# Sliding-window attention in head pairs: eight TensorE jobs per key-value head in place of 26

## The chip, the cores and the metric

The kernel runs on one core of one Trainium2 chip. The metric is the time of one execution in device microseconds (us), as the median of several runs. TensorE does matrix products, VectorE (DVE in the profile) and ScalarE (ACT) do elementwise work and read TensorE's results out of PSUM, GpSimd (POOL) does some elementwise work, and SyncE (SP) issues the DMAs.

## What is computed

One layer of a decoder trunk on 256 tokens of width 2048: a gated DeltaNet branch and a sliding-window attention branch run side by side, are merged by gates, and an MLP follows. The change is in the attention branch alone. Its 32 query heads share 4 key-value heads, 8 to each:

```python
scores = jnp.einsum("bnqkgd,bnskd->bnkgqs", qb, kb).astype(f32) * (SWA_HEAD_DIM ** -0.5)
...
scores = jnp.where(valid[None, :, None, None], scores + bias, -jnp.inf)
sink = sinks.astype(f32).reshape(SWA_KV_HEADS, G)[:, :, None, None]
m = jnp.maximum(scores.max(axis=-1, keepdims=True), sink)
p = jnp.exp(scores - m)
probs = (p / (p.sum(axis=-1, keepdims=True) + jnp.exp(sink - m))).astype(v.dtype)
o = jnp.einsum("bnkgqs,bnskd->bnqkgd", probs, vb)
```

A head is 64 channels wide. The window is 128 tokens, so for one head the 256 queries see three 128x128 blocks of keys: block 0 on itself, block 1 on block 0, block 1 on itself.

## The kernel before

The whole program is one long stream of dense products on TensorE. `output` forms one 256x512 piece of a projection out of 8 (or 16) weight chunks. A chunk is 256x512 weights, loaded by SyncE into a ring of four, then split by ScalarE and VectorE into a high part (`w_hi`, line 648) and a low part (`w_lo`, line 988), three chunks ahead of its use. For each chunk TensorE makes twelve products (lines 288 to 290), six for each of the two 128-row halves. After each half `output` calls a job function with a counter `h`. This counter is the **slot**: a job that belongs to slot h is put into TensorE's stream behind the six products of that slot, and into ScalarE's and VectorE's streams at the same h, behind the split of the chunk that comes three later.

In the stage that the change touches, `mix1`, a loop of four turns over the key-value heads j, each turn is two outputs (a gate projection and the branch product of DeltaNet), which is 32 slots and 192 products, and the attention of the eight heads s of key-value head j is done by `swa_step` in these slots. For one head it has five links:

- **scores** in slot `SCORE[s]`: products 128x128 and 128x256 into PSUM bank `pb` = s mod 2 of `J` (lines 466 and 467). The queries of an even head lie in partitions 0 to 63, those of an odd one in 64 to 127, and each uses the half of the array with those rows.
- VectorE adds the distance bias and takes the maxima (`bias_done`, `negm_done`, lines 1167 to 1174); ScalarE takes the exponentials with their sums (`exps_done`, lines 799 to 802).
- **transposes** in slot `PTURN[s]`: three transposes of `prob` into bank 2 (line 475), which ScalarE copies to `probT` (`pT_copied`, line 805).
- **values** in slot `PV[s]`: three products into bank 3 (lines 483 to 485).
- after an odd head, VectorE divides both heads' results by the sums into `oS` (line 1183, `oS_done`).

Slot 3 transposes the queries of all eight heads (`qfix`), slot 31 the results (`oS`), each by eight transposes (line 317). So TensorE has 3 x 8 + 2 = 26 jobs for each key-value head. Their slots are SCORE = 4, 6, 9, 12, 14, 17, 20, 22; PTURN = 9, 11, 14, 17, 19, 22, 25, 27; PV = 13, 14, 19, 20, 24, 25, 29, 30. Some slots hold two or three of them, and 18 slots of the 32 hold one at least.

The projections use float32r operands (one instruction for each product); the attention's products are float32, of which the trace shows two instructions for each (except for the transposes).

Of the kernel before, what the change touches and what calls it, by code (L numbers as in the profile page):

```python
# [20 lines left out]
ALU = mybir.AluOpType  # L21
ACT = mybir.ActivationFunctionType
F32 = mybir.dt.float32
F32R = mybir.dt.float32r
AX_X = mybir.AxisListType.X

P = 128
T = 256
NT = T // P
# [6 lines left out]
C = 64  # L36
NCH = T // C
U = NT * HG
HQ = 8
# [33 lines left out]
ROWS, TK, TQ, KKQ, INV, QTM, OT = 11, 16, 21, 22, 25, 40, 63  # L73
P1, P2, P3 = (40, 45, 50, 55), (42, 47, 52, 57), (44, 49, 54, None)

SCORE = tuple(4 + 8 * s // 3 for s in range(8))
PTURN = tuple(h + 5 for h in SCORE)
PV = tuple(SCORE[s | 1] + 8 - (s + 1) % 2 for s in range(8))


def hybrid_trunk(nc, x, weights, w_ba, colp_d, rowp_d, masks_d, dist_d, fgain_d, out):
    with ExitStack() as ctx:
# [26 lines left out]
        with ExitStack() as mixers:  # L109
# [17 lines left out]
            with ExitStack() as swa:  # L127
# [4 lines left out]
                qTs = sb("qTs", [P, 4, T], where=swa)  # L132
                kfix = sb("kfix", [P, T], where=swa)
# [132 lines left out]
        def _(pe):  # L266
# [181 lines left out]
            def swa_step(h, j):  # L448
                if h == 3:

                    pe.wait_ge(qfix_done, j + 1)

                    pe.wait_ge(fix_done, j + 1)
                    turn_group(qfix, 0, q_T)
                for s in range(HQ):
                    r = slice((s % 2) * C, (s % 2) * C + C)
                    pb = s % 2
                    if h == SCORE[s]:
                        if s == 0:
                            pe.wait_ge(qT_a, j + 1)  # L460
                            pe.wait_ge(qT_d, j + 1)
                            pe.wait_ge(fix_done, j + 1)
                        if s >= 2:

                            pe.wait_ge(bias_done, HQ * j + (s - 1))
                        mm(J[:, pb, 0:P], qTs[r, s // 2, 0:P], kfix[r, 0:P], start=True, stop=True)  # L466
                        mm(J[:, pb, P:3 * P], qTs[r, s // 2, P:T], kfix[r, 0:T], start=True,  # L467
                           stop=True).then_inc(score_done, 1)
                    if h == PTURN[s]:

                        pe.wait_ge(exps_done, HQ * j + (s + 1))
                        if s:
                            pe.wait_ge(pT_copied, HQ * j + s)
                        for i in range(3):
                            ins = tr(J[:, 2, i * P:(i + 1) * P], prob[:, pb, i * P:(i + 1) * P], ident)  # L475
                        ins.then_inc(p_T, 1)
                    if h == PV[s]:
                        pe.wait_ge(pT_copied, HQ * j + (s + 1))

                        if s and s % 2 == 0:  # L480
                            pe.wait_ge(oS_done, HQ // 2 * j + s // 2)
                        o = J[:, 3, (s % 4) * P:(s % 4 + 1) * P]
                        mm(o[:, 0:C], probT[:, pb, 0:P], vfix[:, 0], start=True, stop=True)
                        mm(o[:, C:P], probT[:, pb, P:2 * P], vfix[:, 0], start=True, stop=False)
                        mm(o[:, C:P], probT[:, pb, 2 * P:3 * P], vfix[:, 1], start=False, stop=True).then_inc(pv_done, 1)
                if h == 31:
                    pe.wait_ge(oS_done, HQ // 2 * (j + 1))
                    turn_group(oS, 0, oS_T)

            def decay_step(h):  # L490
# [145 lines left out]
        def _(act):  # L636
# [146 lines left out]
            def swa_step(h, j):  # L783
                if h == 0:

                    act.wait_ge(sq_d, 4)
                    act.wait_ge(sq_a, 4)
                    A(qfix[:], xres[:, :, bass.ds(j * NB, NB)], ACT.Copy).then_inc(qfix_done, 1)
                if h == 3:
                    act.wait_ge(q_T, j + 1)  # L790
                    A(qTs[:, 0:2], J[:, 0].rearrange("p (a t) -> p a t", a=2), ACT.Copy).then_inc(qT_a, 1)
                for s in range(HQ):
                    pb = s % 2
                    if h == SCORE[s]:
                        act.wait_ge(negm_done, HQ * j + (s + 1))

                        if s >= 2:
                            act.wait_ge(p_T, HQ * j + (s - 1))
                        A(prob[:, pb, 0:P], sbuf_s[:, pb, 0:P], ACT.Exp, bias=negm[:, s, 0:1], accum_out=lsum[:, s, 0:1])
                        A(prob[:, pb, P:3 * P], sbuf_s[:, pb, P:3 * P], ACT.Exp, bias=negm[:, s, 1:2],  # L800
                          accum_out=lsum[:, s, 1:2])
                        A(esink[:, s], negm[:, s], ACT.Exp, bias=slf[:, 1, s:s + 1]).then_inc(exps_done, 1)
                    if h == PTURN[s]:
                        act.wait_ge(p_T, HQ * j + (s + 1))
                        A(probT[:, pb], J[:, 2, 0:3 * P], ACT.Copy).then_inc(pT_copied, 1)
                if h == 31:
                    act.wait_ge(oS_T, j + 1)
                    for b in range(2):
                        ins = A(os_hi[:, bass.ds(j * 4 + 2 * b, 2), :], J[:, b].rearrange("p (a t) -> p a t", a=2), ACT.Copy)
                    ins.then_inc(os_hi_done, 1)  # L810
# [167 lines left out]
        def _(dve):  # L978
# [167 lines left out]
            def swa_step(h, j):  # L1146
                if h == 0:

                    dve.wait_ge(kT_done, 1)
                    dve.wait_ge(kv_d, 1)  # L1150
                    V.tensor_copy(kfix[:], kT[:, bass.ds(j, 1), :].rearrange("p a t -> p (a t)"))
                    V.tensor_copy(vfix[:], vs[:, :, bass.ds(j * C, C)])
                    V.tensor_copy(slf[:], rowp[:, 64:128].rearrange("p (a n) -> p a n", a=2)[:, :, bass.ds(j * HQ, HQ)]).then_inc(fix_done, 1)
                if h == 3:
                    dve.wait_ge(q_T, j + 1)
                    V.tensor_copy(qTs[:, 2:4], J[:, 1].rearrange("p (a t) -> p a t", a=2)).then_inc(qT_d, 1)
                for s in range(HQ):
                    pb = s % 2
                    if h == SCORE[s]:
                        dve.wait_ge(score_done, HQ * j + (s + 1))  # L1160
                        if s == 0:
                            dve.wait_ge(fix_done, j + 1)
                            dve.wait_ge(dist_in, 16)
                        if s >= 2:

                            dve.wait_ge(exps_done, HQ * j + (s - 1))
                        stt(out=sbuf_s[:, pb], in0=dist[:], scalar=slf[:, 0, s:s + 1], in1=J[:, pb, 0:3 * P],
                            op0=ALU.mult, op1=ALU.add).then_inc(bias_done, 1)
                        dve.wait_ge(bias_done, HQ * j + (s + 1))
                        V.tensor_reduce(r3[:, s], sbuf_s[:, pb].rearrange("p (a k) -> p a k", a=3), AX_X, ALU.max).then_inc(max_link, 1)  # L1170
                        dve.wait_ge(max_link, j * (2 * HQ) + (2 * s + 1))
                        tt(r3[:, s, 1:2], r3[:, s, 1:2], r3[:, s, 2:3], ALU.max).then_inc(max_link, 1)
                        dve.wait_ge(max_link, j * (2 * HQ) + (2 * s + 2))
                        ts(negm[:, s], r3[:, s, 0:2], slf[:, 1, s:s + 1], -1.0, ALU.max, ALU.mult).then_inc(negm_done, 1)
                    if h == PV[s] and s % 2:

                        i, pair = s // 2, slice(s - 1, s + 1)
                        dve.wait_ge(pv_done, HQ * j + (s + 1))
                        tt(lsum[:, pair], lsum[:, pair], esink[:, pair], ALU.add).then_inc(l_link, 1)
                        dve.wait_ge(l_link, j * HQ + (2 * i + 1))  # L1180
                        V.reciprocal(lsum[:, pair], lsum[:, pair]).then_inc(l_link, 1)
                        dve.wait_ge(l_link, j * HQ + (2 * i + 2))
                        tt(oS[:, :, (s - 1) * C:(s + 1) * C].rearrange("p t (s c) -> p s t c", s=2),
                           J[:, 3, (s - 1) % 4 * P:((s - 1) % 4 + 2) * P].rearrange("p (s t c) -> p s t c", s=2, t=NT),
                           lsum[:, pair].unsqueeze(3).broadcast_to([P, 2, NT, C]), ALU.mult).then_inc(oS_done, 1)
                if h == 31:
                    dve.wait_ge(os_hi_done, j + 1)
                    for b in range(2):
                        ins = tt(os_lo[:, bass.ds(j * 4 + 2 * b, 2), :], J[:, b].rearrange("p (a t) -> p a t", a=2),
                                 os_hi[:, bass.ds(j * 4 + 2 * b, 2), :].bitcast(F32), ALU.subtract)  # L1190
                    ins.then_inc(os_lo_done, 1)
# [350 lines left out]
```

## Time and profile before

| what | value |
|---|---|
| median of 3 runs | 1968.29 us (1958.04 to 1972.9) |
| the profiled execution, its own time | 1963.88 us |
| its span, first to last instruction | 1962.1 us |
| TensorE busy | 1906.0 us, 97% of the span |
| VectorE busy | 1104.8 us, 56% |
| ScalarE busy | 882.7 us, 45% |
| mean granted clock of TensorE, as a share of full speed | 0.988 |
| the four turns of the stage | 726 to 975 us |

The profiled execution's time is 1.8 us over its span, and 4.4 us under the median of the runs. TensorE's busy time says that it nearly always has a matmul in the array; since matmuls are pipelined, what one costs the stream is read from one start to the next, not from the duration printed.

### The profile page before, as it was taken

What the parts mean: (1) busy time and instruction counts of PE and PEld (TensorE: products, weight loads), DVE (VectorE), ACT (ScalarE), POOL (GpSimd) and SP (SyncE); (2) the same over time, 40 slices, a digit from 0 to 9 for tenths busy, and PEclk for the clock granted to TensorE, in tenths of its full rate; (3) what the DMA queues carried; (4) which work ended last, traced back from release to release, by engine and by line L of the source; (5) the groups of instructions that cost most, each with busy time, mean ns of one, the idle gap of its engine ahead of it and who ended that gap; (6) DMA issues with size and microseconds to landing.
All of it is one profiled execution on the core that took longest, in us unless ns stands there. A gap on an engine that the chain in (4) does not pass through costs nothing.

```text
span 1962.1 us, 29288 instructions
## 1 busy us (share of the span) xinstructions
PE 1906.0 (97%) x10816; PEld 1563.9 (80%) x10816; DVE 1104.8 (56%) x1470; ACT 882.7 (45%) x1398; POOL 120.5 (6%) x86
## 2 busy tenths in 40 slices
PE   7998998998999999999999999999999999999997
PEld 6887877877877888777888888888888888888886
DVE  5366676676676555656555555555554445554444
ACT  5344345354354345455444445444443344444442
POOL 0004014014023000000000000000000000000000
PEclk9899999999999999999999999999999999999999
DMA  6343333333333354344456655555555555555553
GB/s 249 118 165 119 115 130 108 119 119 118 108 127 114 115 165 140 120 138 139 148 194 205 204 200 208 183 184 189 184 192 193 194 192 181 186 188 188 192 195 125
DMA packets 87953, 316.36 MB, mean 161 GB/s; under 512 B 9648, under 2 KB 10160, under 8 KB 87728
## 3 DMA queue, kind: packets, MB, share of 16 engines
q1 hardware_dynamic: 86992, 312.64, 47.2%
q0 software_dynamic: 576, 2.10, 0.3%
q8 instruction: 78, 1.28, 0.2%
q10 hardware_dynamic: 288, 0.18, 0.0%
q14 instruction: 19, 0.16, 0.0%
HBM read 312.79 MB, written 2.10 MB: 160 GB/s over the span
## 4 chain that ended last, share of the span: by engine, by line
PE 54%; issue 38%; DVE 3%; POOL 3%; ACT 1%; DMA 0%; DVEq 0%; ACTq 0%; POOLq 0%; SPq 0%
PE acc L288 15%; PE acc L290 13%; PE acc L289 13%; PE J L385 4%; PE J L433 1%; PE J L317 1%; POOL rg L1406 1%; PE J L424 1%; PE J L467 1%; ACT w_hi L648 1%; PE J L466 1%; PE J L441 1%; DVE cT L1043 1%; DVE qn L1043 1%; PE J L475 1%
## 5 line engine op out<-in xcount | busy, mean ns | idle before, releaser
L988 DVE TENSOR_TENSOR w_lo<-raw,w_hi 128x1024 fp32r<-128x1024 f32 x584 | 724.7, 1243 | 665.8 <-ACT w_hi L648 663.7
L648 ACT ACTIVATE w_hi<-raw 128x1024 fp32r<-128x1024 f32 x584 | 618.3, 1060 | 647.0 <-PE acc L290 645.0
L288 PE MATMUL acc<-w_hi,hT_hi 128*128 128x512 f32 x1440 | 584.6, 406 | 8.4 <-DVE hT_lo L1006 4.5
L290 PE MATMUL acc<-w_hi,hT_lo 128*128 128x512 f32 x1440 | 565.2, 393 | 0.0
L289 PE MATMUL acc<-w_lo,hT_hi 128*128 128x512 f32 x1440 | 565.1, 392 | 0.0
L288 PEld LDWEIGHTS acc<-w_hi,hT_hi 128*128 128x128 f32 x1440 | 272.4, 189 | 74.6 <-issue 11.4
L290 PEld LDWEIGHTS acc<-w_hi,hT_lo 128*128 128x128 f32 x1440 | 272.4, 189 | 59.0
L289 PEld LDWEIGHTS acc<-w_lo,hT_hi 128*128 128x128 f32 x1440 | 272.8, 189 | 52.1 <-issue 1.0
L288 PE MATMUL acc<-w_hi,act_hi 128*128 128x512 f32 x512 | 199.3, 389 | 0.0
L290 PE MATMUL acc<-w_hi,act_lo 128*128 128x512 f32 x512 | 199.2, 389 | 0.0
L289 PE MATMUL acc<-w_lo,act_hi 128*128 128x512 f32 x512 | 199.2, 389 | 0.0
L290 PEld LDWEIGHTS acc<-w_hi,act_lo 128*128 128x128 f32 x512 | 96.1, 188 | 20.1
L288 PEld LDWEIGHTS acc<-w_hi,act_hi 128*128 128x128 f32 x512 | 96.1, 188 | 20.0
L289 PEld LDWEIGHTS acc<-w_lo,act_hi 128*128 128x128 f32 x512 | 96.1, 188 | 19.6
L288 PE MATMUL acc<-w_hi,og_hi 128*128 128x512 f32 x256 | 104.3, 407 | 0.0
L290 PE MATMUL acc<-w_hi,og_lo 128*128 128x512 f32 x256 | 100.2, 391 | 0.0
L289 PE MATMUL acc<-w_lo,og_hi 128*128 128x512 f32 x256 | 99.9, 390 | 0.0
L385 PEld LDWEIGHTS J<-mats 64*64 64x64 f32 x2048 | 66.5, 140 | 24.9 <-issue 24.9
L385 PE MATMUL J<-mats 64*64 64x64 f32 x2048 | 72.6, 226 | 10.6 <-POOL mats L1428 10.6
L288 PEld LDWEIGHTS acc<-w_hi,og_hi 128*128 128x128 f32 x256 | 48.1, 188 | 12.6 <-issue 4.0
L290 PEld LDWEIGHTS acc<-w_hi,og_lo 128*128 128x128 f32 x256 | 48.1, 188 | 10.8
L289 PEld LDWEIGHTS acc<-w_lo,og_hi 128*128 128x128 f32 x256 | 48.2, 188 | 8.7
(210 smaller groups left out, 1565.9 us busy)
## 6 DMA issues: line engine op xcount, KB each, us to landing
raw<-weights SPq DMA_DIRECT2D x584, 512.0 KB, 3.3
xres<-x SPq DMA_DIRECT2D x4, 512.0 KB, 7.8
xres<-x POOLq DMA_DIRECT2D x4, 512.0 KB, 5.7
y<-nat SPq DMA_DIRECT2D x4, 512.0 KB, 2.7
fgain_sb<-fgain SPq DMA_DIRECT2D x1, 1024.0 KB, 5.3
masks_sb<-masks SPq DMA_DIRECT2D x1, 640.0 KB, 11.3
zs<-w_ba SPq DMA_DIRECT2D x1, 256.0 KB, 9.6
dist_sb<-dist SPq DMA_DIRECT2D x1, 192.0 KB, 3.5
```

Source lines behind the costliest of these rows:

```text
L288: mm(o, aT_hi[:, kt, tok], w_hi[:, c % RING, w], start=(c == 0 and k == 0), stop=False)
L289: mm(o, aT_hi[:, kt, tok], w_lo[:, c % RING, w], start=False, stop=False)
L290: last = mm(o, aT_lo[:, kt, tok], w_hi[:, c % RING, w], start=False, stop=(c == nch - 1 and k == CK - 1))
L317: ins = tr(J[:, b0 + m // 2, (m % 2) * T + t * P:(m % 2) * T + (t + 1) * P], src[:, t, m * P:(m + 1) * P], ident)
L385: ins = mm(J[r, bank, u * C:(u + 1) * C], lhs[r, u], rhs[r, u], start=True, stop=True)
L424: ins = mm(J[:, 0, hd * P:(hd + 1) * P], kq[:, hd, c * P:(c + 1) * P], S[:, hd], start=True, stop=True)
L433: ins = mm(J[:, 1, hd * P:(hd + 1) * P], solve[kr, t * HG + hd].rearrange("p a c -> p (a c)"), RH[kr, hd * P:(hd + 1) * P], start=True, st ...
L441: ins = mm(J[:, 2, hd * P:(hd + 1) * P], kn[kr, t, hd * P:(hd + 1) * P], VO[kr, hd * P:(hd + 1) * P], start=True, stop=True)
L466: mm(J[:, pb, 0:P], qTs[r, s // 2, 0:P], kfix[r, 0:P], start=True, stop=True)
L648: A(w_hi[:, slot], raw[:, slot], ACT.Copy).then_inc(hi_ready, 1)
L988: tt(w_lo[:, slot], raw[:, slot], w_hi[:, slot].bitcast(F32), ALU.subtract).then_inc(lo_ready, 1)
L1043: ins = stt(out=dst[:, m, s:T], in0=J[:, b, o:o + T - s], scalar=cwg[:, n, m, 3 - s:4 - s], in1=dst[:, m, s:T], op0=ALU.mult, op1=ALU.add)
```

## The change

The unit becomes a pair of heads (i = 0 to 3, heads 2i and 2i+1). Each kind of job is done for both heads at once: four products for the scores, six transposes, six products for the values, with one semaphore increment for the pair. The transposes use two banks (2 and 3), the values the last quarter of banks 0 and 1. The slots are SCORE = 4, 10, 16, 22; PTURN = 10, 16, 22, 27; PV = 16, 22, 27, 30, so that in slots 16 and 22 the values of one pair, the transposes of the next and the scores of the one after that follow each other directly. Together with slots 3 and 31 this is eight slots with work in place of 18. ScalarE's exponentials get slots of their own, `EXPS`, two behind the scores, and stand one chunk's split later in its stream. VectorE's bias is done for both heads, then one reduction and one maximum for the pair. The values now wait for `bias_done` of the pair after next, since they share its banks.

```diff
-SCORE = tuple(4 + 8 * s // 3 for s in range(8))
-PTURN = tuple(h + 5 for h in SCORE)
-PV = tuple(SCORE[s | 1] + 8 - (s + 1) % 2 for s in range(8))
+PAIRS = HQ // 2
+SCORE, EXPS, PTURN, PV = (4, 10, 16, 22), (6, 12, 18, 24), (10, 16, 22, 27), (16, 22, 27, 30)
...
+                for i in range(PAIRS):
+                    if h == PV[i]:
+                        pe.wait_ge(pT_copied, PAIRS * j + (i + 1))
+
+                        pe.wait_ge(bias_done, PAIRS * j + min(i + 2, PAIRS))
+                        if i:
+                            pe.wait_ge(oS_done, PAIRS * j + i)
+                        for pb in range(2):
+                            o = J[:, pb, 3 * P:4 * P]
+                            mm(o[:, 0:C], probT[:, pb, 0:P], vfix[:, 0], start=True, stop=True)
+                            mm(o[:, C:P], probT[:, pb, P:2 * P], vfix[:, 0], start=True, stop=False)
+                            ins = mm(o[:, C:P], probT[:, pb, 2 * P:3 * P], vfix[:, 1], start=False, stop=True)
+                        ins.then_inc(pv_done, 1)
+                for i in range(PAIRS):
+                    if h == PTURN[i]:
+
+                        pe.wait_ge(exps_done, PAIRS * j + (i + 1))
+                        if i:
+                            pe.wait_ge(pT_copied, PAIRS * j + i)
+                        for pb in range(2):
+                            for b in range(3):
+                                ins = tr(J[:, 2 + pb, b * P:(b + 1) * P], prob[:, pb, b * P:(b + 1) * P], ident)
+                        ins.then_inc(p_T, 1)
...
+                        for pb in range(2):
+                            r = slice(pb * C, pb * C + C)
+                            mm(J[:, pb, 0:P], qTs[r, i, 0:P], kfix[r, 0:P], start=True, stop=True)
+                            ins = mm(J[:, pb, P:3 * P], qTs[r, i, P:T], kfix[r, 0:T], start=True, stop=True)
+                        ins.then_inc(score_done, 1)
...
+                for i in range(PAIRS):
+                    if h == EXPS[i]:
+                        act.wait_ge(negm_done, PAIRS * j + (i + 1))
+
+                        if i:
+                            act.wait_ge(p_T, PAIRS * j + i)
+                        for pb in range(2):
+                            s = 2 * i + pb
+                            A(prob[:, pb, 0:P], sbuf_s[:, pb, 0:P], ACT.Exp, bias=negm[:, s, 0:1], accum_out=lsum[:, s, 0:1])
...
+                for i in range(PAIRS):
+                    if h == PTURN[i]:
+                        act.wait_ge(p_T, PAIRS * j + (i + 1))
+                        A(probT[:], J[:, 2:4, 0:3 * P], ACT.Copy).then_inc(pT_copied, 1)
```

TensorE before, slot 14 of a turn, the fullest of the 18: the values of head 1, the transposes of head 2, the scores of head 4. `J` is the PSUM tile of the attention, `acc` that of the projections; semaphores waited for stand in brackets.

```order
L290 MATMUL acc<-w_hi,hT_lo 128x512
L483 MATMUL J<-vfix,probT 128x64 [waits pT_copied]
L484 MATMUL J<-vfix,probT 128x64
L485 MATMUL J<-vfix,probT 128x64
L475 MATMUL J<-masks_sb,prob 128x128 [waits pT_copied,exps_done]
L475 MATMUL J<-masks_sb,prob 128x128 x2
L466 MATMUL J<-kfix,qTs 128x128 [waits bias_done]
L467 MATMUL J<-kfix,qTs 128x256
L288 MATMUL acc<-w_hi,hT_hi 128x512
```

TensorE now, slot 16: the values of pair 0, the transposes of pair 1, the scores of pair 2.

```order
L463 MATMUL J<-vfix,probT 128x64 [waits bias_done,pT_copied]
L464 MATMUL J<-vfix,probT 128x64
L465 MATMUL J<-vfix,probT 128x64
L463 MATMUL J<-vfix,probT 128x64
L464 MATMUL J<-vfix,probT 128x64
L465 MATMUL J<-vfix,probT 128x64
L475 MATMUL J<-masks_sb,prob 128x128 [waits pT_copied,exps_done]
L475 MATMUL J<-masks_sb,prob 128x128 x5
L488 MATMUL J<-kfix,qTs 128x128 [waits bias_done]
L489 MATMUL J<-kfix,qTs 128x256
L488 MATMUL J<-kfix,qTs 128x128
L489 MATMUL J<-kfix,qTs 128x256
```

The same kinds of work stand in one slot, twice as much of each, and the scores of an odd head follow those of an even one with nothing between them.

ScalarE before, from slot 4 of a turn: each head's exponentials stand between two splits.

```order
L648 ACTIVATE w_hi<-raw 128x1024 [waits chunk_used,raw_in1]
L799 ACTIVATE prob,lsum<-sbuf_s,negm 128x128 [waits negm_done]
L800 ACTIVATE prob,lsum<-sbuf_s,negm 128x256
L802 ACTIVATE esink<-negm,slf 128x2
L648 ACTIVATE w_hi<-raw 128x1024 [waits chunk_used,raw_in2]
L799 ACTIVATE prob,lsum<-sbuf_s,negm 128x128 [waits negm_done]
```

ScalarE now, from slot 4: two splits come first.

```order
L653 ACTIVATE w_hi<-raw 128x1024 [waits chunk_used,raw_in1]
L653 ACTIVATE w_hi<-raw 128x1024 [waits chunk_used,raw_in2]
L805 ACTIVATE prob,lsum<-sbuf_s,negm 128x128 [waits negm_done]
L806 ACTIVATE prob,lsum<-sbuf_s,negm 128x256
L808 ACTIVATE esink<-negm,slf 128x2
L805 ACTIVATE prob,lsum<-sbuf_s,negm 128x128
L806 ACTIVATE prob,lsum<-sbuf_s,negm 128x256
L808 ACTIVATE esink<-negm,slf 128x2
L653 ACTIVATE w_hi<-raw 128x1024 [waits chunk_used,raw_in3]
```

The wait for `negm_done` moved behind the next chunk's split, and six exponentials stand behind one wait in place of three.

## Rows read from the trace of the kernel before

**Rows 1.** The page: busy time of each engine.

```profile
PE 1906.0 (97%) x10816; PEld 1563.9 (80%) x10816; DVE 1104.8 (56%) x1470; ACT 882.7 (45%) x1398; POOL 120.5 (6%) x86
```

**Rows 2.** Timeline of TensorE, slot 3: start, us, engine, line, out<-in.

```profile
726.08 1.03 PE L317 MATMUL J<-masks_sb,qfix 128*128 128x128 f32 x8
726.87 0.48 PE L288 MATMUL acc<-w_hi,hT_hi 128*128 128x512 f32 x1
...
788.36 1.06 PE L317 MATMUL J<-masks_sb,qfix 128*128 128x128 f32 x8
```

**Rows 3.** Timeline of TensorE, slots 4 and 6: scores of head 0 alone.

```profile
728.10 0.39 PE L290 MATMUL acc<-w_hi,hT_lo 128*128 128x512 f32 x1
728.42 0.49 PE L466 MATMUL J<-kfix,qTs 64*128 64x128 f32 x2
728.74 0.59 PE L467 MATMUL J<-kfix,qTs 64*128 64x256 f32 x2
729.27 0.50 PE L288 MATMUL acc<-w_hi,hT_hi 128*128 128x512 f32 x1
729.61 0.39 PE L289 MATMUL acc<-w_lo,hT_hi 128*128 128x512 f32 x1
...
731.90 0.39 PE L290 MATMUL acc<-w_hi,hT_lo 128*128 128x512 f32 x1
```

**Rows 4.** Timeline of TensorE, slot 11: transposes alone.

```profile
741.42 0.49 PE L475 MATMUL J<-masks_sb,prob 128*128 128x128 f32 x3
741.66 0.49 PE L288 MATMUL acc<-w_hi,hT_hi 128*128 128x512 f32 x1
741.99 0.39 PE L289 MATMUL acc<-w_lo,hT_hi 128*128 128x512 f32 x1
```

**Rows 5.** Timeline of TensorE, slot 13: values alone.

```profile
745.58 0.33 PE L483 MATMUL J<-vfix,probT 128*128 128x64 f32 x2
...
746.17 0.48 PE L288 MATMUL acc<-w_hi,hT_hi 128*128 128x512 f32 x1
746.48 0.40 PE L289 MATMUL acc<-w_lo,hT_hi 128*128 128x512 f32 x1
```

**Rows 6.** Timeline of TensorE, slot 14: values, transposes and scores.

```profile
747.64 0.33 PE L483 MATMUL J<-vfix,probT 128*128 128x64 f32 x2
...
748.25 0.50 PE L475 MATMUL J<-masks_sb,prob 128*128 128x128 f32 x3
748.68 0.49 PE L466 MATMUL J<-kfix,qTs 64*128 64x128 f32 x2
...
749.53 0.50 PE L288 MATMUL acc<-w_hi,hT_hi 128*128 128x512 f32 x1
```

**Rows 7.** Timeline of TensorE in the DeltaNet stage: quarter-array products, corners in turn.

```profile
330.57 1.15 PE L385 MATMUL J<-mats 64*64 64x64 f32 x32
331.64 0.50 PE L288 MATMUL acc<-w_hi,hT_hi 128*128 128x512 f32 x1
```

**Rows 8.** Timeline of VectorE and ScalarE behind the scores of head 0.

```profile
729.87 0.61 DVE L1167 SCALAR_TENSOR_TENSOR sbuf_s<-dist_sb,slf,J 128x384 f32<-128x384 f32 x1
...
731.56 0.40 ACT L799 ACTIVATE prob<-sbuf_s,negm 128x128 f32<-128x128 f32 x1 [2.86 <-DVE negm L1174]
...
732.64 1.04 ACT L648 ACTIVATE w_hi<-raw 128x1024 fp32r<-128x1024 f32 x1
```

**Rows 9.** Timeline before slot 31: last `oS`, and the transposes that need it.

```profile
781.02 0.42 DVE L1183 TENSOR_TENSOR oS<-J,lsum 128x256 f32<-128x256 f32 x1
781.86 1.03 PE L317 MATMUL J<-masks_sb,oS 128*128 128x128 f32 x8
```

**Rows 10.** Windows: busy us and instructions of each engine, PEclk, DMA share, GB/s.

```profile
320.00:324.00 4.00, 2.40 (x33) 2.31 (x34) 0.38 (x1) 0.93 (x3) 4.00 (x3) 0.65 0.40 131
...
747.00:751.00 4.00, 4.00 (x23) 3.14 (x22) 1.74 (x4) 2.49 (x7) 0.00 (x0) 1.00 0.52 189
```

**Rows 11.** Waits, 725 to 975 us: total us, times, longest.

```profile
ACT prob L799 <- DVE negm L1174: 91.9, 32, 3.6
```

More of the change, by code:

```diff
@@ L454, in swa_step @@
                     turn_group(qfix, 0, q_T)
[L455 to L459, printed above, removed]
+                for i in range(PAIRS):
[20 more added lines that the diff above has]
+                for i in range(PAIRS):
+                    if h == SCORE[i]:
+                        if i == 0:
                             pe.wait_ge(qT_a, j + 1)
@@ L462, in swa_step @@
                             pe.wait_ge(fix_done, j + 1)
[L463 to L485, printed above, removed]
+                        else:
+                            pe.wait_ge(bias_done, PAIRS * j + i)
+                        for pb in range(2):
[3 more added lines that the diff above has]
+                        ins.then_inc(score_done, 1)
                 if h == 31:
-                    pe.wait_ge(oS_done, HQ // 2 * (j + 1))
+                    pe.wait_ge(oS_done, PAIRS * (j + 1))
                     turn_group(oS, 0, oS_T)
@@ L791, in swa_step @@
                     A(qTs[:, 0:2], J[:, 0].rearrange("p (a t) -> p a t", a=2), ACT.Copy).then_inc(qT_a, 1)
[L792 to L805, printed above, removed]
+                for i in range(PAIRS):
[6 more added lines that the diff above has]
+                            A(prob[:, pb, 0:P], sbuf_s[:, pb, 0:P], ACT.Exp, bias=negm[:, s, 0:1], accum_out=lsum[:, s, 0:1])
+                            A(prob[:, pb, P:3 * P], sbuf_s[:, pb, P:3 * P], ACT.Exp, bias=negm[:, s, 1:2],
+                              accum_out=lsum[:, s, 1:2])
+                            ins = A(esink[:, s], negm[:, s], ACT.Exp, bias=slf[:, 1, s:s + 1])
+                        ins.then_inc(exps_done, 1)
+                for i in range(PAIRS):
+                    if h == PTURN[i]:
+                        act.wait_ge(p_T, PAIRS * j + (i + 1))
+                        A(probT[:], J[:, 2:4, 0:3 * P], ACT.Copy).then_inc(pT_copied, 1)
                 if h == 31:
@@ L1156, in swa_step @@
                     V.tensor_copy(qTs[:, 2:4], J[:, 1].rearrange("p (a t) -> p a t", a=2)).then_inc(qT_d, 1)
[L1157 to L1161, printed above, removed]
+                for i in range(PAIRS):
+                    pair = slice(2 * i, 2 * i + 2)
+                    if h == SCORE[i]:
+                        dve.wait_ge(score_done, PAIRS * j + (i + 1))
+                        if i == 0:
@@ L1162, in swa_step @@
                             dve.wait_ge(fix_done, j + 1)
                             dve.wait_ge(dist_in, 16)
[L1164 to L1178, printed above, removed]
+                        else:
+                            dve.wait_ge(exps_done, PAIRS * j + i)
@@ new lines, in swa_step @@
+                        for pb in range(2):
+                            ins = stt(out=sbuf_s[:, pb], in0=dist[:], scalar=slf[:, 0, 2 * i + pb:2 * i + pb + 1],
+                                      in1=J[:, pb, 0:3 * P], op0=ALU.mult, op1=ALU.add)
+                        ins.then_inc(bias_done, 1)
+                        dve.wait_ge(bias_done, PAIRS * j + (i + 1))
+                        V.tensor_reduce(r3[:, pair], sbuf_s[:].rearrange("p s (a k) -> p s a k", a=3), AX_X, ALU.max).then_inc(max_link, 1)
@@ new lines, in swa_step @@
+                        dve.wait_ge(max_link, j * HQ + (2 * i + 1))
+                        tt(r3[:, pair, 1:2], r3[:, pair, 1:2], r3[:, pair, 2:3], ALU.max).then_inc(max_link, 1)
+                        dve.wait_ge(max_link, j * HQ + (2 * i + 2))
+                        for n in (2 * i, 2 * i + 1):
+                            ins = ts(negm[:, n], r3[:, n, 0:2], slf[:, 1, n:n + 1], -1.0, ALU.max, ALU.mult)
+                        ins.then_inc(negm_done, 1)
+                for i in range(PAIRS):
+                    pair = slice(2 * i, 2 * i + 2)
+                    if h == PV[i]:
+                        dve.wait_ge(pv_done, PAIRS * j + (i + 1))
@@ L1182, in swa_step @@
                         dve.wait_ge(l_link, j * HQ + (2 * i + 2))
-                        tt(oS[:, :, (s - 1) * C:(s + 1) * C].rearrange("p t (s c) -> p s t c", s=2),
-                           J[:, 3, (s - 1) % 4 * P:((s - 1) % 4 + 2) * P].rearrange("p (s t c) -> p s t c", s=2, t=NT),
+                        tt(oS[:, :, 2 * i * C:(2 * i + 2) * C].rearrange("p t (s c) -> p s t c", s=2),
+                           J[:, 0:2, 3 * P:4 * P].rearrange("p s (t c) -> p s t c", t=NT),
                            lsum[:, pair].unsqueeze(3).broadcast_to([P, 2, NT, C]), ALU.mult).then_inc(oS_done, 1)
```

## The prediction

> **What bounds the kernel now.** I read the page first: TensorE is busy for 97% of the span, VectorE for 56%, ScalarE for 45% [rows 1]. Then TensorE's timeline through the attention stage, since a share of busy time doesn't say what a job costs a stream of pipelined matmuls; there I read starts alone. Between jobs a product of the projections starts every 0.229 us (ten steps from 729.61 to 731.90 take 2.29) [rows 3], and each job delays the stream by a fixed time. A turn of the stage, from one transposing of queries to the next, takes 62.28 us [rows 2], of which 192 x 0.229 = 44.0 are the projections; about 18.3 are the jobs and what comes with them. ScalarE waits 91.9 us for the maxima [rows 11], but TensorE doesn't wait for ScalarE behind it. So the stage is bound by TensorE's instruction stream, and the change is worth what it takes out of that stream.
>
> **What a job costs now.** Each price is a start-to-start time, less one step of 0.229.
> - Scores of one head, alone [rows 3]: 728.10 to 728.42 is 0.09 over a step (entry), 0.85 from 728.42 to 729.27 (four instructions), and 0.34 to the next product is 0.11 over a step (exit): 1.05.
> - Three transposes alone [rows 4]: 0.24, exit 0.10: 0.34. Eight take 0.79 [rows 2], 0.099 each, so I count 0.30 for three more.
> - Values of one head alone [rows 5]: 0.59, exit 0.08: 0.67.
> - All three in one slot [rows 6]: 0.61 to the transposes, 0.43 from these to the scores, 0.85, and an exit as above: 2.00. In the 0.43 are 0.24 for the transposes and 0.19 for the change to the scores.
>
> The 18 slots by these prices: the queries 0.79 + 0.08 = 0.87; lone scores in slots 4, 6, 12 make 3.15; transposes with scores (9, 17, 22) 3 x 1.39 = 4.17; lone transposes (11, 27) 0.68; lone values (13, 24, 29, 30) 2.68; slot 14 2.00; values with transposes (19, 25) 2 x 0.95 = 1.90; values with scores (20) about 1.6; the results 0.87. Sum 17.9 us, which stands well to the 18.3 from the period.
>
> **What it costs then.** The work is the same, so each slot is an old one with a second head added, at 0.59 for values, 0.30 for transposes, 0.85 for scores: slot 3 0.87; slot 4 1.05 + 0.85 = 1.90; slot 10 1.39 + 0.30 + 0.85 = 2.54; slots 16 and 22 2.00 + 0.59 + 0.30 + 0.85 = 3.74 each; slot 27 0.95 + 0.59 + 0.30 = 1.84; slot 30 0.67 + 0.59 = 1.26; slot 31 0.87. Sum 16.8. The saving is 1.1 to 1.2 us a turn, 4.6 us in four: entries and exits alone.
>
> **The term that no row shows by itself** is the second head's scores right behind the first's. They use the other half of the array's rows and another bank. The lower bound of the gain is 0: one after the other, as above. If the second head's first instruction can start beside the last of the first head, a pair is shorter by that instruction, (729.27 - 728.74) / 2 = 0.265 us. The upper bound is that all of one head's 0.85 is hidden. The nearest row is that of the 64x64 products, which go to two opposite corners in turn: 32 instructions of 64 columns in 1.07 us, 33 ns each [rows 7]. In the scores' own rows an instruction costs 0.16 us at 128 columns and 0.265 at 256, all in one half, which is 0.05 fixed and 0.05 for each 64 columns: 0.107 for 64 columns, three times the 33 ns. Corners in turn do overlap, so I take 0.265: here the halves change only once in eight instructions. 16 pairs x 0.265 = 4.2 us. The rule behind it, from the Trainium skill, page "TensorEngine Tiling (Array Packing)", section Key Properties: a change of tiling mode drains the array, while different tiles may load weights and multiply in parallel. The trace agrees with the first half (entry 0.09 and exit 0.11 around the half-array products, [rows 3]); by the second the saving is the larger of my two sums, 8.8 instead of 4.6.
>
> **What hides the rest.** VectorE's and ScalarE's work gets fewer instructions or the same; neither sets the end as long as its results come in time. Four places have to hold:
> - Transposes wait for the exponentials. From the start of the bias to ScalarE's start is 1.69 us for a head, and ScalarE takes 1.08 [rows 8]. Doubled in full: 3.4 + 2.2 = 5.5. TensorE gives them six slots (slots 4, 10, 16: 36 x 0.229 = 8.2) and, for the last pair, five slots and the values of pair 2: 6.9 + 1.2 = 8.1. VectorE comes 0.6 late to the scores (729.87 against 729.27) because of its split; a margin of about 2 us stays.
> - The values wait for the copy of the transposes and the bias of the pair after next, both made five or six slots earlier, except slots 27 to 30: three slots, 4.1 us, for one copy of 768 columns.
> - Slot 31 waits for `oS`. Now 0.42 us is to spare (781.44 against 781.86) [rows 9]. Both before and after, the last values stand in slot 30 and the division starts when they end, so this margin stays. It is the thinnest. What is queued behind it on TensorE is the whole next turn.
> - The splits of weights behind VectorE's and ScalarE's longer waits. `w_lo` is made three chunks (six slots, 8.2 us without jobs) ahead; a delay of 3.4 us fits in.
> SyncE's loads hang on `w_lo` and shift by the same few us; nothing else is moved past them. The prologue of a turn (slot 3) is unchanged.
>
> **The sum.** Against the profiled execution, 1963.9 us: less 4.6, less 4.2, gives 1955. The median of the runs is 4.4 above that execution, so the forecast on the median is 1968.3 - 8.8 = 1959.5 us, 0.45% less. The three runs lie 15 us apart, and less than 1% (20 us) is no difference that a measurement of this kernel can tell.
>
> **Rivals.**
> - *No overlap of the heads' halves.* 4.6 us, 1963.7. For it: in the rows of the scores the instructions of one half don't hide their fixed 0.05 at all; only 64-wide corners are seen to overlap, and there the columns differ too. Chance 0.34.
> - *More overlap than one instruction.* If a whole head's scores hide, 16 x 0.85 = 13.6, with 4.6 makes 18.2: 1950. Against it: matmuls start in the order of the stream, and the first head's four come first. Chance 0.07.
> - *The clock falls in the long jobs (slower than before).* In slots 16 and 22 TensorE now does 3.7 us of small float32 work in one piece. In the DeltaNet stage a window of 4 us in which it was busy for only 2.4 had a granted clock of 0.65 [rows 10]. The same for each of the 8 long jobs would cost 0.35 x 4 x 8 = 11.2, net 2.4 slower: 1971. If the products behind each are caught as well, twice that, 1982. Against it: with the 2.0 us job of slot 14 the clock stayed at 1.00, and TensorE was busy throughout [rows 10]; the new jobs have no idle time in them. Chance 0.05.
> - *Transposes wait for exponentials.* It decides from a chain of 8.1 us on, against my 5.5 to 6.1, and outweighs the gain from 8.7: at 9.2 it costs 16 x 1.1 = 17.6, 1977. It would need ScalarE to be held by something that the trace doesn't show. Chance 0.04.
>
> **How the numbers follow.** The forecast has 0.50. Range: from 1950 (the full overlap) to 1970, which takes in no overlap at 1963.7 with the scatter of a median, and the single-priced clock rival's edge. Faster by over 1% only if the full overlap and a lucky median meet: 0.06. Slower by over 1% from the twice-priced clock case and the wait: 0.04. Within 1%: 0.90.
>
> **What the profile after would show.** A turn of 60.0 us in place of 62.3, eight breaks in the stream; the lone score pair of slot 4 at 1.64 us over the steps if halves overlap, 1.90 if not; slots 16 and 22 at 3.5 or 3.7; the clock at 1.00 in the stage; no idle time before the transposes of slot 27 or those of slot 31. I am wrong if a break is longer than its price by a wait (a late `exps_done`, `oS_done`, or `lo_ready`), or if the stage's steps between jobs are no longer 0.229.

## The result and the profile after

The changed kernel takes 1946.02 us in the median of 7 runs (1942.99 to 1954.62), against 1968.29 for the kernel before (1958.04 to 1972.9, 7 runs). The ratio is 0.9907, with a 95% interval from 0.9882 to 0.9932: 18 us less, between 13 and 23. (The two medians alone lie 22 us apart, at the upper end of that interval; this text goes by the ratio, which the turns below bear out.) The forecast was 1959.5, with a range down to 1950; the direction was right and the size was half of what came. The prediction also held that less than 1% (20 us) can't be told on this kernel; with 7 runs each, a change of 0.93% stands clear of no change.

The page of the kernel after, whose span was 1962.1 us before; its second line answers to [rows 1]:

```profile
span 1941.2 us, 29129 instructions
PE 1885.3 (97%) x10816; PEld 1554.7 (80%) x10816; DVE 1099.7 (57%) x1438; ACT 885.4 (46%) x1382; POOL 120.6 (6%) x86
```

TensorE issues the same 10816 matmuls and is busy for 20.7 us less. VectorE and ScalarE hardly changed. (The title sets eight slots against 26 jobs. Counted alike, it is 8 slots in place of 18, or 3 x 4 + 2 = 14 jobs in place of 26.) The timeline of TensorE over two starts of slot 3 (start, duration, as in [rows 2]) shows where the time went:

```profile
723.21 1.03 PE L316 MATMUL J<-masks_sb,qfix 128*128 128x128 f32 x8
...
780.94 1.06 PE L316 MATMUL J<-masks_sb,qfix 128*128 128x128 f32 x8
```

A turn is 57.73 us, 4.55 less than the 62.28 of before; four turns make 18.2. The stage also begins 2.9 us earlier (723.21 against 726.08) in a part that the change doesn't touch. In the runs below this start lies anywhere between 720 and 731 with the same code ahead of it, so it is scatter from one execution to the next, and turns are compared from here on.

Slot 4 of the kernel after, the scores of a pair by themselves. It answers to [rows 3], the scores of one head:

```profile
725.23 0.39 PE L289 MATMUL acc<-w_hi,hT_lo 128*128 128x512 f32 x1
725.55 0.50 PE L488 MATMUL J<-kfix,qTs 64*128 64x128 f32 x4
725.87 0.61 PE L489 MATMUL J<-kfix,qTs 64*128 64x256 f32 x4
726.41 0.50 PE L287 MATMUL acc<-w_hi,hT_hi 128*128 128x512 f32 x1
726.75 0.39 PE L288 MATMUL acc<-w_lo,hT_hi 128*128 128x512 f32 x1
```

The row counts are doubled and the starts are not moved: from the first score instruction to the next projection it is 0.86 us for two heads, where it was 0.85 for one. Slot 16, the fullest, answers to [rows 6]:

```profile
744.40 0.39 PE L289 MATMUL acc<-w_hi,og_lo 128*128 128x512 f32 x1
744.63 0.33 PE L463 MATMUL J<-vfix,probT 128*128 128x64 f32 x2
...
745.91 0.83 PE L475 MATMUL J<-masks_sb,prob 128*128 128x128 f32 x6
746.66 0.50 PE L488 MATMUL J<-kfix,qTs 64*128 64x128 f32 x4
...
747.53 0.50 PE L287 MATMUL acc<-w_hi,og_hi 128*128 128x512 f32 x1
747.86 0.40 PE L288 MATMUL acc<-w_lo,og_hi 128*128 128x512 f32 x1
```

From 744.40 to 747.86, less two steps of 0.229, is 3.00 us (forecast 3.5 with the overlap that it took, 3.74 without). The values are 1.28 for two heads (0.61 for one before), the transposes with the change to the scores 0.75 (0.43), the scores 0.87.

### The profile page after: what moved, and what is told of

Its sections match the earlier page's. It is cut to its first block, busy times and chain, and to the rows that moved or that the text cites. A ratio compares the mean times of both kernels' runs of the same rounds, so it can differ in the third digit from the quotient of the medians.

```text
span 1941.2 us, 29129 instructions
## 1 busy us (share of the span) xinstructions
PE 1885.3 (97%) x10816; PEld 1554.7 (80%) x10816; DVE 1099.7 (57%) x1438; ACT 885.4 (46%) x1382; POOL 120.6 (6%) x86
## 3 DMA queue, kind: packets, MB, share of 16 engines
q8 instruction: 78, 1.28, 0.3%
## 4 chain that ended last, share of the span: by engine, by line
PE 53%; issue 38%; DVE 3%; POOL 3%; ACT 1%; DMA 0%; DVEq 0%; ACTq 0%; POOLq 0%; SPq 0%
PE acc L287 15%; PE acc L289 14%; PE acc L288 14%; PE J L384 4%; PE J L432 1%; PE J L316 1%; POOL rg L1418 1%; PE J L423 1%; ACT w_hi L653 1%; PE J L440 1%; DVE cT L1051 1%; DVE qn L1051 1%; PE J L475 1%; PE J L304 0%; POOL mats L1440 0%
```

## The experiments

Turn below means the time from the first to the second start of slot 3 in the timeline of TensorE; it is 62.28 us for the kernel before and 57.73 for the changed kernel. In the three profiled executions of the changed kernel it came out as 57.73 or 57.72.

**Both heads on one half of the rows.** The questions were whether the second head's scores are free because they use the other half of the array, and what they cost otherwise.

```diff
                         for pb in range(2):
-                            r = slice(pb * C, pb * C + C)
+                            r = slice(0, C)
                             mm(J[:, pb, 0:P], qTs[r, i, 0:P], kfix[r, 0:P], start=True, stop=True)
```

> The changed kernel, with one edit: the scores of the second head of a pair read the queries and keys of partitions 0 to 63 too, so all score products use the same half of the array's rows, at the same place, number and size. The scores of odd heads are therefore those of the head before. Theory A (the two halves of the rows run side by side, and a pair costs what one head cost, 0.85 us): a pair now costs 1.70, 16 pairs x 0.85 = 13.6 us more than the changed kernel, a turn of 61.0 us in place of 57.6, time about 1957. Theory B (the pair is cheap because like products stand next to each other, whatever half they use): no difference from the changed kernel, 1943 to 1946.

Measured: 1956.53 us (1953.33 to 1961.42), ratio to before 0.9958 [0.994, 0.9975]; a turn of 60.29, 2.56 more than the changed kernel, 0.64 a pair. Slot 4 in its timeline:

```profile
725.80 0.49 PE L488 MATMUL J<-kfix,qTs 64*128 64x128 f32 x2
726.13 0.59 PE L489 MATMUL J<-kfix,qTs 64*128 64x256 f32 x2
726.56 0.38 PE L488 MATMUL J<-kfix,qTs 64*128 64x128 f32 x2
726.78 0.59 PE L489 MATMUL J<-kfix,qTs 64*128 64x256 f32 x2
727.30 0.50 PE L287 MATMUL acc<-w_hi,hT_hi 128*128 128x512 f32 x1
```

Theory B falls: with neighbours of the same form, but on one half, 2.56 of the gain of 4.55 us a turn is gone. The other 1.99 stays, and is what fewer and longer jobs give without the halves. Theory A holds, with a smaller price. The four products take 1.50 us, not 1.70: two take 0.86 and two more 0.64. In the middle, 726.56 to 726.78 is 0.22 for two instructions of 128 columns and 726.13 to 726.56 is 0.43 for two of 256, which is 0.11 us for each 128 columns and nothing fixed. So of the 0.85 that one head costs, 0.64 is its columns, and 0.21 belongs to the job: 0.11 in the first product and 0.09 in the last, on top of the entry of 0.09 and the exit of 0.11.

**The scores of a pair apart.** The same slots and the same work, but another kind of product between the two heads' scores.

```diff
+                for i in range(PAIRS):
+                    if h == SCORE[i]:
...
+                        scores(i, 0)
                 for i in range(PAIRS):
                     if h == PTURN[i]:
...
+                for i in range(PAIRS):
+                    if h == SCORE[i]:
+                        scores(i, 1).then_inc(score_done, 1)
```

> The changed kernel, with one edit of order: in slots 10, 16 and 22 the scores of the first head stand ahead of the six transposes and those of the second behind them; slot 4 is unchanged. Theory A: in 12 pairs of 16 the halves can't overlap, each costs 0.85 and one more entry and exit of about 0.2, so 12 x 1.05 = 12.6 us more, slot 16 at 4.05 us over its steps in place of 3.0, slot 4 still at 1.06; time about 1956. Theory B gives the same for slots 10 to 22, since the products are no longer neighbours. Theory C (the gain came from fewer slots alone, wherever the products stand in them): less than 3 us more.

Measured: 1960.74 us (1952.35 to 1966.13), ratio to before 0.9981 [0.9964, 0.9998]; a turn of 60.74, 3.01 more than the changed kernel, 1.0 for each of the three pairs that are split. Slot 16, from the timeline:

```profile
751.97 0.39 PE L465 MATMUL J<-vfix,probT 128*128 128x64 f32 x2
752.28 0.48 PE L469 MATMUL J<-kfix,qTs 64*128 64x128 f32 x2
752.61 0.59 PE L470 MATMUL J<-kfix,qTs 64*128 64x256 f32 x2
753.13 0.87 PE L490 MATMUL J<-masks_sb,prob 128*128 128x128 f32 x6
753.94 0.48 PE L469 MATMUL J<-kfix,qTs 64*128 64x128 f32 x2
754.26 0.59 PE L470 MATMUL J<-kfix,qTs 64*128 64x256 f32 x2
754.79 0.50 PE L287 MATMUL acc<-w_hi,og_hi 128*128 128x512 f32 x1
```

Each head's scores now take 0.85 (752.28 to 753.13, and 753.94 to 754.79), and each change of shape adds about 0.1. Theory C falls with it: eight slots alone, without the neighbourhood, leave 1.54 of the 4.55 us a turn, and in that the undivided pair of slot 4 still has its overlap.

**Only the scores in pairs.** The other way round, from the kernel before: nothing but three lines of slots.

```diff
-SCORE = tuple(4 + 8 * s // 3 for s in range(8))
-PTURN = tuple(h + 5 for h in SCORE)
-PV = tuple(SCORE[s | 1] + 8 - (s + 1) % 2 for s in range(8))
+SCORE = (4, 4, 10, 10, 16, 16, 22, 22)
+PTURN = (9, 10, 15, 16, 21, 22, 26, 27)
+PV = (12, 13, 18, 19, 24, 25, 29, 30)
```

> The kernel before, with only the slots changed: SCORE = 4, 4, 10, 10, 16, 16, 22, 22, transposes and values one head at a time in slots of their own (PTURN 9, 10, 15, 16, 21, 22, 26, 27; PV 12, 13, 18, 19, 24, 25, 29, 30). 19 slots hold work, one more than before. Theory A: the scores alone carry most of the gain. By the prices of lone jobs the slots sum to 14.0 us a turn in place of 17.9, 3.9 x 4 = 15.5 us less than before, ratio 0.992. If pairs of scores didn't overlap it would be 17.4, about 2 us less. Theory C (fewer slots make the gain): no gain.

Measured: 1951.24 us (1948.14 to 1953.36), ratio to before 0.9927 [0.9902, 0.9953]; a turn of 58.33, 3.95 less than before. With 19 slots in use and transposes and values as scattered as ever, this gives 3.95 of the 4.55 us a turn. The rest of the change, its slots of transposes and values in pairs and all its new semaphore counts, is worth 0.6 us a turn, 2.4 in all.

**The order within a pair.**

```diff
                             mm(J[:, pb, 0:P], qTs[r, i, 0:P], kfix[r, 0:P], start=True, stop=True)
+                        for pb in range(2):
+                            r = slice(pb * C, pb * C + C)
                             ins = mm(J[:, pb, P:3 * P], qTs[r, i, P:T], kfix[r, 0:T], start=True, stop=True)
```

> The changed kernel, with the four score products of a pair in the order: first head 128 columns, second head 128 columns, first head 256, second head 256. Theory A with no regard to order (each half takes its own products as it comes free): a pair stays at 0.85 us, a turn at 57.6. Theory A with the order of the stream kept would have made the changed kernel's own order slower than this one, so a gain here of some 0.3 us a pair would speak for it.

Measured, in a single run: 1948.51 us and a turn of 57.70 against 57.73. The order of the four products makes no difference, so the engine finds the second half's work behind the first half's by itself.

**How far it looks.** Each score product twice, all of one half ahead of all of the other.

```diff
-                        for pb in range(2):
+                        for n in range(4):
+                            pb = n // 2
                             r = slice(pb * C, pb * C + C)
```

> The changed kernel, with each score product of a pair issued twice, in the order first head, first head, second head, second head: all four products of one half of the rows stand ahead of those of the other. The run with both heads on one half gave 0.64 us for each further head and 0.21 fixed for the job. Theory A with free lookahead over a whole half: a pair costs 0.21 + 2 x 0.64 = 1.49 us in place of 0.85, slot 4 at 1.70 over its steps, 10.2 us more than the changed kernel. If the engine looks less far ahead than four products (eight instructions with their weight loads), part of the second half's work comes behind: up to 0.21 + 4 x 0.64 = 2.77, slot 4 at up to 2.98.

Measured, in a single run: 1972.73 us, a turn of 63.36, 5.63 more than the changed kernel, 1.41 a pair. Slot 4:

```profile
732.83 0.49 PE L489 MATMUL J<-kfix,qTs 64*128 64x128 f32 x2
733.16 0.59 PE L490 MATMUL J<-kfix,qTs 64*128 64x256 f32 x2
733.59 0.49 PE L489 MATMUL J<-kfix,qTs 64*128 64x128 f32 x4
733.81 0.70 PE L490 MATMUL J<-kfix,qTs 64*128 64x256 f32 x4
734.36 0.38 PE L489 MATMUL J<-kfix,qTs 64*128 64x128 f32 x2
734.58 0.59 PE L490 MATMUL J<-kfix,qTs 64*128 64x256 f32 x2
735.10 0.50 PE L287 MATMUL acc<-w_hi,hT_hi 128*128 128x512 f32 x1
```

The counts tell it: x2, x4, x2. There are three rounds in place of two (all side by side) or four (none): the first two products of one half run alone, the next two run beside the first two of the other half, and the last two run alone. So the other half's work is found behind two products of one half (four instructions), as in the changed kernel, but not behind four (eight). Where between these the limit lies, and what sets it, these runs don't tell. The cost is 2.27 us; three rounds at 0.64 and the job's 0.21 would be 2.13.

**The same means for the values.** If halves of the rows run side by side for whole jobs, halves of the columns may too. The values are made turned: 64 columns of v as weights, the transposed shares as 128 moving columns, one head into partitions 0 to 63 and the other into 64 to 127. Then `oS` and the eight transposes of slot 31 aren't needed, but VectorE has to divide the shares before they are transposed.

```diff
+SHARE = (8, 14, 20, 26)
...
-                        for pb in range(2):
-                            o = J[:, pb, 3 * P:4 * P]
-                            mm(o[:, 0:C], probT[:, pb, 0:P], vfix[:, 0], start=True, stop=True)
...
+                        for blk, t, first, last in ((0, 0, True, True), (1, 0, True, False), (2, 1, False, True)):
+                            for pb in range(2):
+                                ins = mm(J[pb * C:pb * C + C, min(blk, 1), 3 * P:4 * P], vfix[:, t],
+                                         probT[:, pb, blk * P:(blk + 1) * P], start=first, stop=last)
...
-                if h == 31:
-                    pe.wait_ge(oS_done, PAIRS * (j + 1))
-                    turn_group(oS, 0, oS_T)
...
+                    if h == SHARE[i]:
+                        dve.wait_ge(exps_done, PAIRS * j + (i + 1))
...
+                        for pb in range(2):
+                            ts(prob[:, pb, 0:P], prob[:, pb, 0:P], lsum[:, 2 * i + pb, 0:1], None, ALU.mult)
+                            ins = ts(prob[:, pb, P:3 * P], prob[:, pb, P:3 * P], lsum[:, 2 * i + pb, 1:2], None, ALU.mult)
```

> The changed kernel, carried further by the same means: the values of a pair are made turned (64 weight columns of v, 128 moving columns of the transposed shares), the first head into PSUM partitions 0 to 63 and the second into 64 to 127, in turn, so that two halves of the array's columns can run side by side. VectorE divides the shares by their sums ahead of the transposes (slots 8, 14, 20, 26) and makes both parts of the result from PSUM; the eight transposes of slot 31 are gone. Theory A extended to column halves: values of a pair at 0.21 + 0.64 with an entry and exit of 0.2, 1.05 in place of 1.34 when alone, 4 x 0.29 = 1.2 us a turn, and 0.88 for slot 31: 2.0 a turn, 8 us less than the changed kernel, about 1938. If column halves don't overlap: values at 1.7 alone, 1.4 more a turn less 0.88, 2 us slower than the changed kernel. If VectorE's six more operations a pair make the transposes wait, slower still, to be seen as idle time before them.

> The changed kernel once more, on the chip and in the rounds of the one before it, as its measure: 1943 to 1950, 20 us less than the kernel before.

Measured: 1944.5 us (1940.62 to 1950.13), ratio to before 0.9896 [0.9876, 0.9915]; the changed kernel beside it 1945.59, 0.9899 [0.9882, 0.9916]. No difference between them can be told. A turn is 57.22, 0.51 less. Where the 2 us a turn went stands in this kernel's timeline: the values of slot 30, then slot 10, then slot 27.

```profile
777.67 0.88 PE L464 MATMUL J<-probT,vfix 128*64 128x128 f32 x12
778.48 0.50 PE L288 MATMUL acc<-w_hi,og_hi 128*128 128x512 f32 x1
```

```profile
736.90 1.04 ACT L650 ACTIVATE w_hi<-raw 128x1024 fp32r<-128x1024 f32 x1
737.98 1.23 DVE L988 TENSOR_TENSOR w_lo<-raw,w_hi 128x1024 fp32r<-128x1024 f32 x1 [2.13 <-ACT w_hi L650]
...
739.12 0.15 DVE L1191 TENSOR_TENSOR lsum<-lsum,esink 128x4 f32<-128x4 f32 x1
...
739.49 0.39 PE L290 MATMUL acc<-w_hi,hT_lo 128*128 128x512 f32 x1
...
740.18 0.35 DVE L1197 TENSOR_SCALAR prob<-prob,lsum 128x256 f32<-128x256 f32 x1
...
740.59 0.87 PE L475 MATMUL J<-masks_sb,prob 128*128 128x128 f32 x6 [0.71 <-DVE prob L1197]
```

```profile
771.12 0.88 PE L464 MATMUL J<-probT,vfix 128*64 128x128 f32 x12
772.77 0.88 PE L475 MATMUL J<-masks_sb,prob 128*128 128x128 f32 x6 [0.78 <-DVE prob L1197]
```

Columns do overlap: the twelve instructions take 0.81 us (the values of a pair 1.25 to 1.28 before), and one by one in the trace they start in pairs, 5 to 7 ns apart, with 0.11 us from one pair to the next after the first. (The shape of the products changed too, and no run has the turned values on one half of the columns; the starts in pairs are what shows the overlap.) But the transposes wait for VectorE. The exponentials end when ScalarE turns to its split, at 736.90; VectorE waits for that split, makes its own (737.98 to 739.21) and divides the shares only then. From start to start the wait is 0.87 us in slot 10 (739.49 to 740.59 is 1.10, a step 0.23) and 0.84 in slot 27 (771.12 to 772.77 is 1.65, the values 0.81). That is 1.7 a turn, more than the 1.3 which the next expectation states, and it takes most of what the turned values give.

**The shares earlier.**

```diff
-SHARE = (8, 14, 20, 26)
+SHARE = (7, 13, 19, 25)
```

> The kernel with the turned values, with one edit: VectorE divides the shares one slot earlier (7, 13, 19, 25), ahead of the split of weights that it made first. In the run before, that split (1.23 us) stood between the end of the exponentials and the division, and the transposes of slots 10 and 27 began 0.8 and 0.5 us late. Theory: both waits go, 1.3 us a turn, 5.4 us in all: a turn of 55.8 us in place of 57.2, slot 10 at 1.75 over its steps, time about 8 us under the changed kernel, ratio to the kernel before about 0.986. Rival: the wait returns in the split, which now comes later for a chunk that is nearly due; then breaks appear between projections.

> The changed kernel as the measure of the one before it, on the same chip: 1943 to 1948, ratio 0.990.

Measured: 1938.2 us (1930.53 to 1941.48), ratio to before 0.9856 [0.9829, 0.9883]; the changed kernel beside it 1947.82 (1939.89 to 1951.79), 0.991 [0.9885, 0.9934]. So this kernel is 9.6 us under the changed kernel in the medians, which its turn bears out: 55.41, 2.32 less, 9.3 in four turns. Against the kernel with the late shares the turn is 1.81 us shorter, 7.2 in four turns; the expectation had 1.3 and 5.4, because it read the waits too small. Its slot 10:

```profile
734.75 0.39 PE L290 MATMUL acc<-w_hi,hT_lo 128*128 128x512 f32 x1
734.98 0.82 PE L475 MATMUL J<-masks_sb,prob 128*128 128x128 f32 x6
735.73 0.50 PE L488 MATMUL J<-kfix,qTs 64*128 64x128 f32 x4
...
736.59 0.50 PE L288 MATMUL acc<-w_hi,hT_hi 128*128 128x512 f32 x1
```

The transposes follow the projection after one step of 0.23; the wait is gone, and none came up in the splits. So the turned values and the missing slot 31 are together worth 2.3 us a turn, where 2.0 was expected.

## Why the prediction was wrong

**What bounds the stage** was right: TensorE's stream, with prices read from start to start. The eight breaks are there, projections still step by 0.229 us, and the prices, read again in the new timeline, add up: the eight breaks sum to 13.8 us, and 57.73 less 44.0 for the projections is 13.8 (57.73 - 192 x 0.229).

**The steps that failed are the two prices of the second head's scores.** The sum had two terms for the stage, 4.6 us for fewer entries and exits and 4.2 for overlap, and both were too small.

- *"each slot is an old one with a second head added, at ... 0.85 for scores"*. The 0.85 of [rows 3] is 0.64 for the columns and 0.21 for the job, which a second head in the same job doesn't pay again. The kernel with both heads on one half is the one in which only this term is at work: 62.28 - 60.29 = 1.99 us a turn, 8.0 in four, in place of 4.6. What was mis-sized is the job's part, 16 x 0.21 = 3.4 us. That this is the whole difference is luck, since smaller terms nearly cancel beside it. The second head's values and transposes cost more than taken, about 1.6 us in all. Against that, the jobs of the kernel before sum to 18.1 us a turn and not 17.9, and outside the jobs a turn takes 44.2 us before and 43.9 with both heads on one half, which no price holds; together about 2 us. The row that would have told of the job's part stood in the same group: the two instructions of 128 columns and the two of 256 take 0.32 and 0.53, a difference of 0.21 for 256 columns, which is 0.11 for each 128; I spread the remainder over the four instructions as a fixed 0.05 each. A job with more instructions of that kind, had I priced one, would have shown whether the remainder grows.
- *"so I take 0.265"*, because *"matmuls start in the order of the stream"*. This was the reason given against the rival of full overlap, and no row of the profile before carried it. In the changed kernel the four instructions of 128 columns all start in 725.55 to 725.8, ahead of the first head's 256 columns (725.87), though the second head's come later in the stream. What overlaps is the whole second head: 0.64 x 16 = 10.2 us in place of 4.2, and 60.29 - 57.73 = 2.56 a turn says the same.

Together 8.0 + 10.2 = 18.2 us, which is what four turns gained, and what the ratio says. The rival of full overlap, at 0.07, had the mechanism, and its figure of 18.2 holds because a pair did cost 0.86 where a head cost 0.85. But of its 13.6 only 10.2 is overlap; the other 3.4 are the job's part, which is saved without it. That the rest then came to its 4.6 owes to the small terms above.

The small prices: values for a second head 0.67 (taken 0.59), three more transposes 0.32 (taken 0.30). Both are 0.11 us an instruction, the pace of 128 columns in the scores, though the values have 64 moving columns.

**The rules weighed.** The page "TensorEngine Tiling (Array Packing)" of the Trainium skill, section Key Properties, says that different tiles run in parallel, which the runs bear out for halves of the rows and of the columns. The other half of the rule, that a change of tiling mode drains the array, is less well borne out than the prediction has it. The entry of 0.09 us does stand only ahead of jobs on half the array (the full-array values of slot 16 start one plain step of 0.23 behind the projection, 744.40 to 744.63). But an exit of 0.08 to 0.10 stands behind full-array transposes and values too [rows 4, rows 5], so the 0.11 behind the scores says little. What I took to speak against a full overlap was my own reading of how the queue works; the same skill's page "TensorE: Matmul & The Clock Gate", section "Part 3: Packing small matmuls — row/col tiling", has matmuls start strictly in program order. Here the measurement decides: the second head's 128 columns began before the first head's 256.

**The cover held.** The places that could have brought a wait didn't: in the waits of the kernel after, TensorE waits for no exponentials, and ScalarE's wait for the maxima, 91.9 us before [rows 11], is down to this:

```profile
ACT prob L805 <- DVE negm L1185: 2.2, 4, 0.6
```

That the longer chain was near a limit all the same was shown by the kernel with the turned values, where 1.4 us more on VectorE (739.12 to 740.53), behind a split, became up to 0.87 of waiting in a slot.

**The clock** stayed. The window that holds slot 16 of the kernel after, in the columns of [rows 10]:

```profile
744.00:748.00 4.00, 4.00 (x32) 3.34 (x31) 1.57 (x2) 2.49 (x4) 0.00 (x0) 1.00 0.43 131
```

The job of 3.0 us of small products without idle time had no effect on the granted clock; the rival of the falling clock is out for this kernel.

## What to carry to other kernels

Small products that use one half of the array's rows or columns belong next to their counterpart of the other half, in one job: for the scores the second cost nothing, while the same two jobs apart cost twice, and three lines of slots were enough for seven eighths of this gain. Keep the run on one half short: with two products on each half the two overlapped in full, with four only half of them did. Price a job by what the second instruction of a kind adds, not by the job's length over its count: here a quarter of a lone job was paid once per job. And when such a merge lengthens another engine's chain, look for what stands ahead of that chain's link in its engine's stream; moving one step ahead of one weight split was worth 7 us.

## What the runs showed of the hardware

- Four float32 products of 64 rows, two on each half of the rows, took 0.86 us, as two on one half did (0.85); four on one half took 1.50.
- The second half's products were found behind two of the first half's (four instructions) and not behind four (eight); the order of the four within a pair made no difference (57.70 against 57.73 us a turn).
- A lone float32 job of scores on half the rows cost 0.41 us beyond its columns: entry 0.09, exit 0.11, and 0.21 within it. Full-array jobs had no such entry (0.00), but an exit of 0.08 to 0.10.
- Twelve instructions with 64 weight columns and 128 moving ones, alternating between the halves of the columns, took 0.81 us, where the same values with 128 weight columns and 64 moving ones took 1.28.
